# Decay levels of a gated linear-attention scan: half of the exponent differences computed on GpSimd, half on VectorE

## The reference, cut to what matters

```python
b = jnp.cumsum(fb, axis=2)
diff = b[:, :, :, None, :] - b[:, :, None, :, :]
decay = jnp.exp(jnp.where(incl, diff, -jnp.inf))
scores = jnp.einsum('nhtk,nhsk,nhtsk->nhts', qb, kb, decay)
intra = jnp.einsum('nhts,nhsv->nhtv', scores, vb)
```

## Time and profile before

| | |
|---|---|
| median of 3 runs | 1709.61 us (1707.3 to 1710.12) |
| the profiled execution | 1711.76 us; its span, first to last instruction, 1710.0 us |
| granted TensorE clock, mean | 0.962 |
| busy: TensorE, GpSimd, VectorE, ScalarE | 1630.0, 1208.4, 1028.3, 808.8 us |
| the level stage, level 0 to level 17 | 662.7 to 768.8 us of the span |

### The profile page before, as it was taken

How to read it: one execution, slowest core, us unless ns; L and a number is a source line. 1 busy time by engine, 2 the same in 40 slices (tenths; PEclk the granted TensorE clock), 3 DMA queues, 4 the chain that set the end, 5 groups by cost and what they waited for, 6 DMA issues and landing times.

```text
span 1710.0 us, 31420 instructions
## 1 busy us (share of the span) xinstructions
PE 1630.0 (95%) x11688; PEld 1472.5 (86%) x11688; DVE 1028.3 (60%) x1358; ACT 808.8 (47%) x1078; POOL 1208.4 (71%) x504
## 2 busy tenths in 40 slices
PE   6888999999999999889999999999999999999997
PEld 5666779999899888888989999999999888888886
DVE  4633338666421168983415997177777999974344
ACT  5423355545655457654444444444444434444543
POOL 5830238888688595445875899877777777778995
PEclk9996599999999999988999999999999999999999
DMA  7431046555555334222654554554544455465553
GB/s 267 132 119 47 1 148 234 185 185 185 168 181 179 123 125 134 88 75 89 207 199 135 183 180 162 180 166 156 162 157 164 157 167 168 163 210 195 194 190 120
DMA packets 72629, 268.41 MB, mean 157 GB/s; under 512 B 8160, under 2 KB 8432, under 8 KB 71344
## 3 DMA queue, kind: packets, MB, share of 16 engines
q1 hardware_dynamic: 70128, 253.99, 45.2%
q0 software_dynamic: 1568, 7.66, 1.3%
q10 hardware_dynamic: 864, 5.77, 0.9%
HBM read 264.24 MB, written 3.15 MB: 156 GB/s over the span
## 4 chain that ended last, share of the span: by engine, by line
PE 38%; issue 25%; POOL 25%; DVE 5%; ACT 4%; DMA 2%; POOLq 0%; SPq 0%; DVEq 0%; ACTq 0%
PE ps L1095 38%; POOL ring_lo L1154 24%; DMA ring<-in_stream 2%; DVE big L859 1%; ACT ring_hi L1556 1%; DVE big L858 1%; DVE big L884 1%; ACT big L600 0%; ACT big L605 0%; DVE big L857 0%; ACT big L630 0%; DVE big L868 0%; DVE big L860 0%; ACT h_hi L1569 0%; POOL big L1188 0%
## 5 line engine op out<-in xcount | busy, mean ns | idle before, releaser
L1154 POOL TENSOR_TENSOR ring_lo<-ring,ring_hi 128x1024 fp32r<-128x1024 f32 x472 | 1183.7, 2523 | 479.8 <-ACT ring_hi L1556 478.7
L1556 ACT CAST ring_hi<-ring 128x1024 fp32r<-128x1024 f32 x472 | 489.7, 1050 | 479.2 <-DMA ring<-in_stream 476.9
L1095 PE MATMUL ps<-h_hi,ring_hi 128*128 128x256 f32 x2144 | 616.5, 288 | 8.3 <-POOL ring_lo L1154 5.0
L1095 PE MATMUL ps<-h_lo,ring_hi 128*128 128x256 f32 x2144 | 610.3, 285 | 0.0
L1095 PE MATMUL ps<-h_hi,ring_lo 128*128 128x256 f32 x2144 | 610.1, 285 | 0.0
L1095 PEld LDWEIGHTS ps<-h_hi,ring_hi 128*128 128x128 f32 x2144 | 414.7, 193 | 12.8 <-issue 9.2
L1095 PEld LDWEIGHTS ps<-h_lo,ring_hi 128*128 128x128 f32 x2144 | 414.7, 193 | 0.8 <-issue 0.5
L1095 PEld LDWEIGHTS ps<-h_hi,ring_lo 128*128 128x128 f32 x2144 | 414.5, 193 | 0.0
L1095 PE MATMUL ps<-ring_hi,h_hi 128*128 128x512 f32 (+1 forms) x672 | 266.6, 397 | 14.8 <-POOL ring_lo L1154 8.9
L1095 PE MATMUL ps<-ring_hi,h_lo 128*128 128x512 f32 (+1 forms) x672 | 262.1, 390 | 0.0
L1095 PE MATMUL ps<-ring_lo,h_hi 128*128 128x512 f32 (+1 forms) x672 | 261.8, 390 | 0.0
(11 more groups left out here) (313 smaller groups left out, 1552.6 us busy)
## 6 DMA issues: line engine op xcount, KB each, us to landing
ring<-in_stream SPq DMA_DIRECT2D x480, 512.0 KB, 3.6
residual<-big ACTq DMA_DIRECT2D x2, 1024.0 KB, 4.0
big<-residual ACTq DMA_DIRECT2D x2, 1024.0 KB, 7.9
x<-in_x SPq DMA_DIRECT2D x1, 1024.0 KB, 5.6
big<-in_fdecay POOLq DMA_DIRECT2D x1, 1024.0 KB, 9.4
wrow<-in_post POOLq DMA_DIRECT2D x2, 512.0 KB, 6.5
big<-in_x ACTq DMA_DIRECT2D x1, 1024.0 KB, 5.0
big<-in_dft POOLq DMA_DIRECT2D x1, 1024.0 KB, 10.1
```

The costliest lines, as they stand in the source:

```text
L1095: return nc.tensor.matmul(out, lhsT, rhs, start=start, stop=stop, skip_group_check=True)
L1154: P.tensor_tensor(ring_lo[:, h % RING, :], ring[:, h % RING, :], ring_hi[:, h % RING, :].bitcast(fp32), ALU.subtract).then_inc(S["split_lo ...
L1556: A.copy(ring_hi[:, h % RING, :], ring[:, h % RING, :]).then_inc(S["split_hi"], 1)
```

## The change

The two backward differences (lines 858 and 859) leave VectorE for GpSimd, where `backward_differences(n)` issues them between the low parts; VectorE keeps the two forward ones. ScalarE's exponential of the keys now waits for one difference of each engine, and so does that of the queries. The order of GpSimd's instructions is written out: low parts up to half 169, the pair of level 1, halves 170 and 171, the pair of level 2, halves 172 and 173, the pairs of levels 3 and 4, two low parts, the pairs of 5 and 6, two low parts, the pair of 7, and the same for the second group.

```diff
-            rests(2 * W_FFN + 6, 2 * W_Q + 6)
+            rests(2 * W_FFN + 6, 2 * W_OG + 2)
+
+            def backward_differences(n):
+
+                hg, m = n // 9, 128 >> (n % 9)
+                pool.wait_ge(S["keys_ready"], 4 * hg + 6)
+                if n >= 2:
+                    pool.wait_ge(S["level_product"], n - 1)
+                keys, queries = (split_view(LV[n % 2][:, part, :], m) for part in range(2))
+                kb, d = (level_view(a, hg, m) for a in (KB, DB))
+                d_first = d[:, :, 1, 0:1].broadcast_to([128, 512 // m, m])
+                P.tensor_tensor(keys[:, :, 1, :], kb[:, :, 1, :], d_first, ALU.subtract).then_inc(S["pool_step"], 1)
+                P.tensor_tensor(queries[:, :, 0, :], d_first, d[:, :, 0, :], ALU.subtract).then_inc(S["pool_step"], 1)
+
+            for n in range(1, NLV):
+                if n % 9 not in (0, 8):
+                    backward_differences(n)
+                if n == 1:
+                    rests(2 * W_OG + 2, 2 * W_OG + 4)
+                if n % 2 == 0 and n < 16:
+                    rests(2 * W_OG + n + 2, 2 * W_OG + n + 4)
+            rests(2 * W_OG + 18, 2 * W_Q + 6)
...
-                        act.wait_ge(S["level_shifted"], 4 * exponent_steps(n) - 2 + 2 * part)
+                        act.wait_ge(S["level_shifted"], 2 * exponent_steps(n) - 1 + part)
+                        act.wait_ge(S["pool_step"], 5 + 2 * exponent_steps(n) - 1 + part)
...
-                V.tensor_tensor(keys[:, :, 1, :], kb[:, :, 1, :], d_first, ALU.subtract).then_inc(S["level_shifted"], 1)
-                V.tensor_tensor(queries[:, :, 0, :], d_first, d[:, :, 0, :], ALU.subtract).then_inc(S["level_shifted"], 1)
```

More of the change, by code:

```diff
@@ L852, in exponents @@
                 keys, queries = (split_view(LV[n % 2][:, part, :], m) for part in range(2))
-                kf, kb, f, d = (level_view(a, hg, m) for a in (KF, KB, BF, DB))
+                kf, f = (level_view(a, hg, m) for a in (KF, BF))
                 offsets = f if n == 1 else level_view(SUMS, 0, m)
                 nb = 512 // m
-                f_last, d_first = offsets[:, :, 0, m - 1:m].broadcast_to([128, nb, m]), d[:, :, 1, 0:1].broadcast_to([128, nb, m])
+                f_last = offsets[:, :, 0, m - 1:m].broadcast_to([128, nb, m])
                 V.tensor_tensor(keys[:, :, 0, :], kf[:, :, 0, :], f_last, ALU.add).then_inc(S["level_shifted"], 1)
-                V.tensor_tensor(keys[:, :, 1, :], kb[:, :, 1, :], d_first, ALU.subtract).then_inc(S["level_shifted"], 1)
-                V.tensor_tensor(queries[:, :, 0, :], d_first, d[:, :, 0, :], ALU.subtract).then_inc(S["level_shifted"], 1)
                 V.tensor_tensor(queries[:, :, 1, :], f[:, :, 1, :], f_last, ALU.subtract).then_inc(S["level_shifted"], 1)
```

## The result

The change takes 1717.66 us (median of 20 runs, 1705.79 to 1722.37) against 1709.77 us for the kernel before in the same sessions (20 runs). The ratio is 1.0044 with a 95% interval of 1.0028 to 1.0060: slower by 5 to 10 us. The forecast was 1718 us within 1711 to 1733, and slower.

What follows compares the result with a forecast made beforehand. TensorE bounds the kernel (95% busy), but in the levels' stage a loop through three engines has VectorE late from turns with GpSimd. Terms +4.9, +2.4, +3.8, -2.9 sum to +8.2 us: 1718 us, range 1711 to 1733.

Steps and rivals of the forecast that it cites:

- up to level 2: Stage start to level 2: GpSimd's pairs queue behind low parts, level 2 starting at 679.8 instead of 674.95, +4.9 us.
- levels 2 to 6: Stage steps: even-to-odd lengthened by two low parts, then the pair, on GpSimd; 27.8 against 25.4 us, +2.4 us.
- levels 6 to 11: Stage steps from level 6 to 11: 33.6 against 29.8 us, the last step carrying most, +3.8 us.
- level 11 to the second values product: End of the stage: takes 39.1 us instead of 42.0, -2.9 us.
- The price: Each 128x512 backward difference on GpSimd: 1.27 us, from a straight line between 128x640 and 128x1024; the sum hangs on it.
- a sign of being wrong: Backward differences on GpSimd: pairs above 1.5 us would show the forecast wrong.
- The rival of short rows: Differences on GpSimd: short runs make each cost 1.5 to 1.9 us, giving +12 to +23 us; chance 0.18.
- the wait for line 573: Between level 11 and the second values product: a wait of 3.6 us shrinks to some 2 us.
- 15 to 16: Step from level 15 to 16: 0.9 us shorter.
- the end: Before the second values product: 1.0 us longer, VectorE's line 1770 standing behind low parts 186 and 187.
- The forecast said for GpSimd and not for VectorE: Sign of being right, in the stage: ScalarE's line 652 waits for GpSimd, not for VectorE.
- The faster rival: In the stage: taking turns was the bound, so 12 of 15.7 us TensorE idle time goes, giving 1698; chance 0.07.

Runs made afterwards that it cites:

- two pairs ahead: The change, with the pairs of levels 1 and 2 put on GpSimd ahead of the two low parts they stood behind: 1714.45 us, ratio 1.0024 to the kernel before.

## Why the prediction was right

The four terms of its sum, each as the difference between the change's steps and those of the earlier trace rows:

| stretch | forecast, us | measured, us |
|---|---|---|
| up to level 2 | +4.9 | 16.0 - 12.2 = +3.8 |
| levels 2 to 6 | +2.4 | 28.3 - 25.4 = +2.9 |
| levels 6 to 11 | +3.8 | 33.35 - 29.8 = +3.6 |
| level 11 to the second values product | -2.9 | 38.5 - 42.0 = -3.5 |
| sum | +8.2 | +6.8 |

The mechanism was right for the first three terms: the pairs behind the low parts, found in the order of the queue and not in the load of an engine. The fourth came out near its number by luck. What was off:

**The price, at both ends.** The forecast took 1.27 us for every level, from a line through two other sizes. Those of the first pair took 1.05 us each, those of level 5 1.27, line 309 of levels 6 and 7 1.5. Seven of the 28 were above 1.5 us, which the prediction named as a sign of being wrong, three of them held by VectorE's product with Q. It did not decide, since the high ones made up for the low ones: all 28 together took 17.4 + 18.5 = 35.9 us, and 28 x 1.27 is 35.6. At levels 1 and 2 four differences are in line, and 4 x 0.22 = 0.9 of the missing 1.1 us is this. The Trainium skill's figure (GPSIMD Engine Reference, Elementwise, side-by-side cycle accounting) gives an estimate of 1.12 us in proportion, which was nearer to the first levels than the line was; the spacing of starts, 664.64 to 665.65, gives 1.01. For blocks of 8 and 4, and for line 309 below that, both are too low. The rival of short rows was half true: both lines get dearer down to blocks of 4, by 0.22 us, and below that line 309 alone, by 0.47 in all. How far the sum really hangs on the price the prediction doesn't settle: it gives +6.4 for 1.0 us and for 1.19 us alike.

**The last term was right in size and mostly not in its reasons.** The reasons that it names add up to -1.6 (the wait for line 573), -0.9 (15 to 16) and +1.0 (the end), which is -1.5; for the other 1.4 us of its -2.9 it gives none. Of the -3.5 measured, 2.7 us are the clock: from the first values product to level 13 the kernel before took 13.8 us and the change 11.1, because TensorE ran the 16 values products and level 12 at the full clock of 2.4 GHz, 5.50 us against 8.22 (granted clock 1.00 against 0.66). The wait did shrink, from 3.60 to 1.42 us, but level 11 before it took 3.54 us instead of 1.95, at a granted clock of 0.55, so that step gained only 0.6. 15 to 16 was 0.85 shorter, as said; 13 to 15 was 0.7 longer, and the end was as long as before (8.0 us from level 16) and not 1.0 longer. Without the row at the full clock the term would have been -0.8 and the sum +9.5. The forecast had no term for the clock.

**ScalarE waits for GpSimd only at the odd levels and level 2.** The forecast said for GpSimd and not for VectorE. At the other even levels the wait is for line 879 (11.4 us): the forward difference stands behind line 888 on VectorE, and was hidden only at odd levels.

**The faster rival** had the right size (12 us of idle time) and was given 0.07 because the order put the pair after the low parts. Turned round, the order gives 12.0 us, 2.7 of them in the row at the full clock. It was the place that separated it from the forecast.

That the time came out 0.3 us from the forecast is luck beyond this: the sum was 1.4 us too high, the stage lost 6.8 us, the profiled executions differ by 7.0, and the medians by 7.9 with an interval of 5 us.

## What to carry to other kernels

When work moves to an engine with time to spare, look at what stands in front of it in that engine's queue, and what those instructions wait for; a share of 47.5 of 103 us busy says nothing about that. Put the short work for which others wait ahead of the long work that is needed later, and check by the deadlines of the long work that it can stand it. If VectorE's instructions differ in length by the place of one operand, count what the turns with GpSimd cost before moving anything: an operand in PSUM gave as much here as a whole reordering. That kernel read the forward offset for both directions; a second copy in PSUM, for the backward one, was not tried (the forward one takes VectorE 1.23 us).

## What was not expected of the hardware

A subtraction of 128x512 elements on GpSimd depends on the length of its runs in steps that differ between two instructions of the same shape. In the changed kernel, undisturbed: runs of 64: 1.05 and 1.05 us; of 16: 1.11 and 1.14; of 8: 1.17 and 1.16; of 4: 1.27 and 1.27; of 1: 1.52 for line 309 and 1.04 for line 310. With runs of 2 it is 1.51 and 1.03, at level 15:

```profile
762.17 1.51 POOL L309 TENSOR_TENSOR big<-big 128x512 f32<-128x512 f32 x1
763.65 1.03 POOL L310 TENSOR_TENSOR big<-big 128x512 f32<-128x512 f32 x1
```

At levels 6, 14 and 16 line 310 took 2.02, 2.26 and 2.02 us. Each of these began 0.1 to 0.3 us behind a product with Q on VectorE. Line 309 is the keys' difference, line 310 the queries'. Both have the same counts and strides. The keys' reads and writes the second block of each pair, the queries' writes the first, and the repeated offset is the second input of the one and the first of the other. Which of these makes the difference was not tried.

The granted clock over the stretch from 662 to 765 us was 0.93 before, 0.95 in the change although it idled more, and 0.88 with two pairs ahead. One row of 32 products alone took from 5.50 us (granted clock 1.00) to 8.54 (0.64), and the waits of TensorE just before it do not sort the cases: 3.60 us of wait came before 8.22, 2.80 before 5.50, 2.02 before 8.54. These 3 us are as much as several of the terms above.
